# Two attentions of a diffusion trunk: scores of a later unit ahead of a pair's value products, and modulation columns read one step later

## The reference, cut to what matters

```python
# first block: for each of 4 heads two score maps, p = softmax(s0) - lam * softmax(s1)
s = einsum('bqhmd,bkhmd->bhmqk', qi, k) * scale
p = einsum('bhmqk,m->bhqk', softmax(s, axis=-1), w)
out = einsum('bhqk,bkhd->bqhd', p, v)
# second block: 8 heads, local scores with a bias, context scores without; then 4 heads of the plain kind
s_loc = einsum('brqhd,brkhd->bhrqk', qg, kg) * scale + bias[None]
p = softmax(concatenate([s_loc, s_ctx], axis=-1), axis=-1)
# each block also needs six modulation vectors, mod = silu(c) @ w_mod[l] + b_mod[l]
```

## Time and profile before

| | us |
|---|---|
| median of 3 runs | 1896.15 (1895.96 to 1896.84) |
| the profiled execution | 1897.83 |
| its span on the core | 1895.9 |
| PE busy | 1827.2 (96%) |
| DVE busy | 1260.8 (66%) |
| ACT busy | 1074.7 (57%) |
| share of the chain that ended last | PE 91%, DVE 4%, ACT 2% |
| first attention, first scores to last value product | about 177 to 222.5 |
| second attention, the same | 795.9 to 853.0 |

### The profile page before, as it was taken

The page is one execution under the profiler, slowest core; times in us unless marked ns, Lnnn a source line. Parts: engine busy times, 40 slices in busy tenths (PEclk is TensorE's granted clock), DMA queues, the critical chain, the costliest instruction groups (busy, mean ns, idle before and its releaser), DMA issues.

```text
span 1895.9 us, 23206 instructions
## 1 busy us (share of the span) xinstructions
PE 1827.2 (96%) x9612; PEld 1483.7 (78%) x9612; DVE 1260.8 (66%) x1189; ACT 1074.7 (57%) x1098; POOL 26.0 (1%) x27
## 2 busy tenths in 40 slices
PE   6998898999999989989999999999999999999998
PEld 4876576888888868658888888888888888888886
DVE  4343726222233363273888889889898898988987
ACT  5332635222232254364777777777777777777775
POOL 0000000000000001120000000000000000000000
PEclk9998998999999989999899999999999999999999
DMA  9653225533232262444999999999999999999994
GB/s 336 189 179 111 65 92 163 170 102 98 89 110 91 89 217 78 113 127 146 328 369 371 367 377 333 368 380 364 366 339 371 375 360 378 330 379 366 361 373 177
DMA packets 263216, 473.89 MB, mean 250 GB/s; under 512 B 16120, under 2 KB 115376, under 8 KB 263104
## 3 DMA queue, kind: packets, MB, share of 16 engines
q1 hardware_dynamic: 262720, 471.38, 70.6%
q0 software_dynamic: 384, 0.95, 0.2%
HBM read 471.25 MB, written 1.05 MB: 249 GB/s over the span
## 4 chain that ended last, share of the span: by engine, by line
PE 91%; DVE 4%; ACT 2%; issue 1%; SPq 1%; DMA 1%; ACTq 0%; DVEq 0%
PE bank L543 27%; PE bank L545 27%; PE bank L544 27%; PE bank L610 2%; PE bank L2195 1%; PE bank L2158 1%; PE bank L400 1%; PE bank L618 1%; DMA raw_weights<-in_ev_w_in 1%; ACT split_high L522 1%; SPq L1088 1%; PE bank L816 0%; PE bank L924 0%; PE bank L898 0%; DVE small L966 0%
## 5 line engine op out<-in xcount | busy, mean ns | idle before, releaser
L1686 DVE TENSOR_TENSOR split_low<-raw_weights,split_high 128x2048 fp32r<-128x2048 f32 x224 | 513.0, 2290 | 42.6 <-ACT split_high L1431 41.7
L1431 ACT ACTIVATE split_high<-raw_weights 128x2048 fp32r<-128x2048 f32 x222 | 426.1, 1920 | 139.6 <-PE bank L545 139.6
L527 DVE TENSOR_TENSOR split_low<-raw_weights,split_high 128x1024 fp32r<-128x1024 f32 x118 | 144.1, 1226 | 293.6 <-ACT split_high L522 293.6
L543 PE MATMUL bank<-h_high,split_high 128*128 128x512 f32 (+1 forms) x832 | 318.0, 382 | 8.0 <-DVE h_low L457 4.2
L544 PE MATMUL bank<-h_low,split_high 128*128 128x512 f32 (+1 forms) x832 | 315.1, 379 | 0.0
L545 PE MATMUL bank<-h_high,split_low 128*128 128x512 f32 (+1 forms) x832 | 314.6, 378 | 0.0
L1686 DVE TENSOR_TENSOR h_low<-raw_weights,h_high 128x2048 fp32r<-128x2048 f32 x112 | 256.8, 2293 | 54.3 <-ACT h_high L1431 53.3
L543 PE MATMUL bank<-split_high,xe_high 128*128 128x512 f32 x672 | 266.4, 396 | 0.0
L545 PE MATMUL bank<-split_high,xe_low 128*128 128x512 f32 x672 | 262.3, 390 | 0.0
L544 PE MATMUL bank<-split_low,xe_high 128*128 128x512 f32 x672 | 262.0, 390 | 0.0
L1431 ACT ACTIVATE h_high<-raw_weights 128x2048 fp32r<-128x2048 f32 x112 | 214.9, 1919 | 50.2 <-PE bank L545 50.2
(11 more groups left out here) (281 smaller groups left out, 2437.6 us busy)
## 6 DMA issues: line engine op xcount, KB each, us to landing
raw_weights<-in_moe_w SPq DMA_DIRECT2D x336, 1024.0 KB, 7.2
raw_weights<-in_w_mod SPq DMA_DIRECT2D x48, 1024.0 KB, 6.2
raw_weights<-in_ffn_w SPq DMA_DIRECT2D x33, 1024.0 KB, 5.3
raw_weights<-in_ev_w_in SPq DMA_DIRECT2D x10, 1024.0 KB, 10.3
raw_weights<-in_od_w_in SPq DMA_DIRECT2D x8, 1024.0 KB, 8.8
raw_weights<-in_ev_w_out SPq DMA_DIRECT2D x4, 1024.0 KB, 6.6
raw_weights<-in_od_w_out SPq DMA_DIRECT2D x4, 1024.0 KB, 8.2
overlay<-in_rpb SPq DMA_DIRECT2D x32, 64.0 KB, 3.0
```

The source lines that it names most:

```text
L527: dve.tensor_tensor(half_of(s, j, SPL[:, s % NSPLIT, :]), half_of(s, j, raw_of(split_at[s])), half_of(s, j, SPH[:, s % NSPLIT, :]).bitcast ...
L543: pe.matmul(ps, wh, xh, start=first, stop=False)
L1431: act.activation(esplit(u)[0], RAW[:, u % NRAW, :], ACT.Copy).then_inc(S("e_high"), 1)
L1686: dve.tensor_tensor(lo, RAW[:, u % NRAW, :], hi.bitcast(F32), ALU.subtract).then_inc(S("e_low"), 1)
```

## The change

In both attentions PE still issues scores(i+1) at the head of step i, but only if they weren't issued before. In the odd steps from 3 on, the scores of unit i+2 are issued just ahead of the value product. So the scores of units 5, 7, 9, 11, 13 and 15 move from behind a value product to ahead of it; the even units' scores stay where they were. On DVE, in the second attention, `dve_mods` (line 682) moves from step 3 to step 4.

```diff
@@ pe_attention1
+            scored = 2
             for i in range(1, len(att1) + 2):
-                if i + 1 < len(att1):
+                if i + 1 < len(att1) and i + 1 == scored:
                     scores(i + 1)
+                    scored += 1
...
                 between(i)
                 if i >= 3 and i % 2 == 1:
+                    if i + 2 < len(att1):
+                        scores(i + 2)
+                        scored += 1
                     p = (i - 2) // 2
@@ pe_attention: the same with len(units)
@@ dve_between
-                if i == 3:
+                if i == 4:
                     dve_mods(dve, 9, 10, 6)
```

More of the change, by code:

```diff
@@ L903, in pe_attention @@
             scores(1)
+            scored = 2
             for i in range(1, len(units) + 2):
-                if i + 1 < len(units):
+                if i + 1 < len(units) and i + 1 == scored:
                     scores(i + 1)
+                    scored += 1
                 if i <= len(units):
@@ L917, in pe_attention @@
                 if i >= 3 and i % 2 == 1:
+                    if i + 2 < len(units):
+                        scores(i + 2)
+                        scored += 1
                     p = (i - 2) // 2
```

## The result

The changed kernel takes 1899.67 us in the median of 18 runs (1896.13 to 1904.69), the kernel before 1896.66 in 18 runs beside it (1894.64 to 1900.93). The ratio is 1.0017, with a 95% interval from 1.0011 to 1.0024: about 3.2 us slower, clear of noise, but within the 0.2% that the prediction called the same. The time lies in its range (1893.8 to 1900.2) and on the side of the forecast (1897.6), but about twice as far from before as forecast (+1.5), and outside the forecast's own range (1896.3 to 1898.9).

The account below looks back on a forecast made before the run. The prediction took PE as holding 91% of the last-ending chain, with DVE the fuller engine in the first attention. +2.4 - 0.7 - 0.2 = +1.5 us on 1896.15 gave 1897.6, range 1893.8 to 1900.2 (the forecast's own 1896.3 to 1898.9).

Parts of the forecast that it names:

- Part 1: First attention: later value products delay DVE's copies, 0.79 us in each of three periods, +2.4 us (bounds 1.8 to 3.0).
- Rival D: First attention: longer PE waits let the granted clock fall, +6 on top of +1.5, 1903.6 us; chance 0.08.
- Part 2: Second attention: modulation columns a step later let unit 3's bias start 2.0 us sooner; -0.7 us, bounds -4.1 and +1.3.
- unit 2's and unit 3's pairs: Second attention: DVE's two line 877 probability instructions per unit meet GpSimd's masking and take 2 to 3 us a pair.
- Part 3: Second attention: moved scores remove one DVE wait (0.6 us) but add 0.4 us from unit 10's stretch on; -0.2 us.
- A: First attention: earlier scores pay in full, copies not held, -2.0 in place of +2.4, 1893.3 us; chance 0.06.
- B: Second attention: DVE and GpSimd no longer meet, Part 2 gives -3.5, in all -1.3, 1894.9 us; chance 0.18.
- C: Second attention: one more pair is hit by GpSimd, Part 2 becomes +1.3, in all +3.5, 1899.7 us; chance 0.11.

Follow-up runs that it names:

- order alone: The kernel before with the new order of scores in the first attention only; ratio to before 1.0021, +4.0 us.
- order with later copy: The changed kernel with the first attention's copy of line 986 one step later on DVE (lag 4, not 3); ratio to before 0.9976.
- later copy alone: The kernel before with the first attention's copy one step later on DVE and nothing else; ratio to before 0.9996.
- columns alone: The kernel before with only `dve_mods` (the modulation columns) a step later; ratio to before 1.0000, second attention 57.35 us.
- masking cut short: The changed kernel with GpSimd's masking cut to one column of each tile in place of 64, run once; second attention 54.2 us.
- filler: The changed kernel with the first attention's scores of units 4, 8 and 12 multiplied three times in place of once; ratio to before 1.0017.

## Why the prediction was right, and where its sizes were off

*What bounds.* Right. The row on which the argument turned was the product's end at 193.31 against the copy's start at 193.35. The chain of waits named the scores; the engine that would be late next was in the row before.

*Part 1.* The mechanism is shown by its three kernels (order alone, order with later copy, later copy alone). Its size was forecast at 0.37 + 0.42 = 0.79 us a period and measured at 1.0 (10.73 against 9.73). The term mis-sized is the value product: taken at 1.03 and 1.89 us, it took 1.13 and 1.99 behind scores, 0.10 more in each of six. That possibility stood in the sum only as the upper bound; it should have been the value, since in the earlier trace rows no product stands behind 64-row scores, and so no row bore out the lower figure there.

*Rival D, the clock.* It was given 0.08 and a price of +6. It did happen, in each unfilled profile of this order: in two of the four once, for 1.1 and 1.4 us with 1.2 given back in the tail, in the other two twice, for 2.5 us and 1.1 more in the tail. None comes near +6, whose 3.2 us a period also isn't the sum of the terms it names (1.89 + 2 x 1.13 = 4.15). The step that failed was the price for all three periods, and the chance: that the wait ahead of transposes 6 would grow from 1.56 to 2.05 was worked out rightly (2.03), and what a wait of 2.19 us had done in the tail of before should have counted for more.

*Part 2.* Forecast -0.7 us; the columns alone gave -0.68 in the second attention. That unit 2's and unit 3's pairs would meet GpSimd (near 11.5 - 8.8 = 2.7 us for the first) was right in kind: 1.99 and 1.90 in one profile of the changed kernel, 2.82 and 2.24 in another. In the first profile less was lost than forecast, in the second about as forecast. The forecast's own terms give 0.5 rather than 0.7: 0.2 of the first pair, and 0.3 because the second is held for 0.7 + 1.04 in place of 2.08.

*Part 3.* Forecast -0.2, measured about 0 (57.33 with, 57.35 without). Gain and loss were both somewhat larger: units 10 to 15 cost 0.6 and not 0.4, so the others must have gained about as much.

*Sum.* +3.0 for +2.4, about -0.7 for -0.9, and a share of the clock's falls that was not in the sum. That is +2.3 and the rest, against 3.2 measured with an interval from 2.1 to 4.6. Part 1's +3.0 was the upper bound of the forecast, worked out for this very cause. That the time came inside the range even so, with falls of the clock that no term held, is in part luck.

*Rivals A, B and C.* A is out: all six copies concerned were held. B, that DVE and GpSimd no longer meet, is out; with masking cut short it would have been worth 2.1 us. C, a third pair held, came in no profile: unit 4's pair took 0.91 and 0.88 us in the changed kernel's two. Its time of 1899.7 is the nearest to the measured 1899.67, by coincidence.

## What to carry to other kernels

When something is moved ahead of a piece of work, look not only at who waits for what is moved but at how close behind the piece its reader stands; a reader that starts 0.04 us after the end is already the next bound, though no view lists it as a wait. Move the reader with the work: here the order alone lost 4 us, the later copy alone did nothing, and both together gained 4.6. Where two engines share something that one holds for a whole instruction, shifting one of them by 2 us gives only what the next meeting leaves (0.7 us in the profile); to halve the other one's work gave 1.4 (one profile each). And a gain that one profile shows in a stretch is not yet a gain of the kernel: here a stretch further on took 1.6 us longer, at a lower mean clock, in four of twelve.

## What the runs showed of the hardware

A value product of 128-row tiles takes 0.10 us longer right behind scores of 64-row tiles (1.13 against 1.03, 1.99 against 1.89) wherever the clock stayed up in the profiles of the new order.

The granted clock fell to its lower level behind waits of PE of 2.03 to 2.66 us in the first attention, and not behind waits of 0.57 to 1.56 us. With filler that cut the wait to 0.63 it stayed up, and fell at the next long wait instead. Not every wait of that size did it: in the changed kernel's second profile 2.03 us ahead of transposes 10 and 2.66 ahead of transposes 14 were followed by value products of 1.13 and 1.03 us, and in the kernel before 2.22 us in the second attention left the transposes at 1.09 us, their time at the full clock. Nor does the slow work start right behind the wait: in the first profile the waits of 2.03 ahead of transposes 6 and of 2.66 ahead of transposes 14 were followed by transposes of 0.66 us and only then by slow rows.

VectorE's instruction of 512 columns, 0.47 us alone, is held about 1.1 us by each instruction of GpSimd that it meets, and takes 1.5 us in all. The Trainium skill (SBUF — State Buffer, "SBUF: two separate sides") has this as an exclusive lock on a shared port pair, held for the whole instruction by whoever starts first. The runs agree on the hold. On who gets it they don't where both start within 0.1 us: at 807.33 GpSimd leads VectorE's 807.41 and wins, as the rule has it, but in the earlier trace rows VectorE's 813.99 leads 814.03 and loses.
